# Small recurrence products as 64-column tiles, and expert tiles of 80 slots

## The reference, cut to what matters

```python
def moe_swiglu(xn, w_router, w_gate, w_up, w_down):
    xt = xn.reshape(-1, d)                        # 256 rows
    logits = (xt @ w_router).astype(jnp.float32)
    top_vals, top_idx = lax.top_k(logits, TOP_K)  # 2 of 8 experts
    ...
    for e in range(N_EXPERTS):                    # widths 1024 -> 3584 -> 1024
        y = y + combine[:, e:e + 1] * swiglu(xt, w_gate[e], w_up[e], w_down[e])

def step(state, inp):                             # the recurrence, a state of 64 x 64 per head
    sa = jnp.einsum('bhvk,bhk->bhv', state, -kk_t)
    state = (state * w_t[:, :, None, :] + sa[..., None] * (kk_t * a_t)[:, :, None, :]
             + v_t[..., None] * k_t[:, :, None, :])
    return state, jnp.einsum('bhvk,bhk->bhv', state, r_t)
```

## Time and profile before

| | |
|---|---|
| median of 3 runs | 3103.71 us (3098.95 to 3111.47) |
| the profiled execution | 3109.32 us, its span 3107.6 us |
| TensorE busy | 2872.6 us, 92% of the span |
| TensorE weight loads busy | 2470.1 us, 79% |
| VectorE, ScalarE busy | 795.6 us, 427.0 us |
| mean granted clock | 0.943 |
| read from device memory | 568.79 MB |

### The profile page before, as it was taken

One profiled execution on the slowest core, in us unless ns is written; L12 is line 12 of the kernel. 1 busy time (PEld: TensorE's weight loads), 2 busy tenths in 40 slices (PEclk: granted clock), 3 DMA queues, 4 the chain that ended last, 5 costly groups with the idle time before them and its releaser, 6 DMA issues. The chain is left out here.

```text
span 3107.6 us, 71912 instructions
## 1 busy us (share of the span) xinstructions
PE 2872.6 (92%) x31985; PEld 2470.1 (79%) x31985; DVE 795.6 (26%) x1962; ACT 427.0 (14%) x941; POOL 84.3 (3%) x144
## 2 busy tenths in 40 slices
PE   8798999979799999999999898999788999997998
PEld 6687776768699999999999777665677889896665
DVE  5412000621201101101110123000436766763001
ACT  1101000111101100101000122000023222221000
POOL 0100000000000000000000000000000000001000
PEclk9899999989899999999999976999898988988999
DMA  6334445433399999999999630645300000001442
GB/s 211 121 110 136 149 149 159 142 109 127 110 399 381 390 408 390 388 407 389 389 407 390 220 109 7 204 156 191 115 19 4 3 3 2 2 2 61 143 154 95
DMA packets 291364, 571.02 MB, mean 184 GB/s; under 512 B 18182, under 2 KB 181764, under 8 KB 291284
## 3 DMA queue, kind: packets, MB, share of 16 engines
q1 hardware_dynamic: 291284, 569.92, 50.9%
HBM read 568.79 MB, written 5.28 MB: 185 GB/s over the span
## 5 line engine op out<-in xcount | busy, mean ns | idle before, releaser
L1604 PE MATMUL ps<-xg,ring 128*64 128x88 f32 x14336 | 549.7, 239 | 1.1 <-issue 1.1
L1604 PEld LDWEIGHTS ps<-xg,ring 128*64 128x64 f32 x14336 | 545.7, 137 | 2.8 <-issue 2.8
L1199 PE MATMUL ps<-xT,ring 128*128 128x256 f32 x1728 | 386.0, 383 | 5.2 <-PEq L445 2.5
L1199 PEld LDWEIGHTS ps<-xT,ring 128*128 128x128 f32 x1728 | 332.5, 193 | 68.7 <-issue 22.0
L1211 PE MATMUL ps<-ring,hidden 128*128 128x512 f32 x688 | 301.8, 592 | 0.0
L1620 PE MATMUL ps<-hidden,expert_down 128*64 128x88 f32 x7168 | 277.8, 239 | 2.1 <-issue 2.1
L1620 PEld LDWEIGHTS ps<-hidden,expert_down 128*64 128x64 f32 x7168 | 274.2, 137 | 2.5 <-issue 2.5
L1211 PEld LDWEIGHTS ps<-ring,hidden 128*128 128x128 f32 x688 | 130.7, 190 | 147.5 <-issue 145.4
L610 PE MATMUL ps<-ring,xT 128*128 128x256 f32 (+1 forms) x1056 | 229.0, 380 | 8.0 <-PEq L1080 5.5
L610 PEld LDWEIGHTS ps<-ring,xT 128*128 128x128 f32 x1056 | 198.8, 196 | 36.7 <-issue 9.7
L610 PE MATMUL ps<-xT,ring 128*128 128x256 f32 (+1 forms) x944 | 212.9, 387 | 9.9 <-PEq L588 4.5
(11 more groups left out here) (354 smaller groups left out, 2641.7 us busy)
## 6 DMA issues: line engine op xcount, KB each, us to landing
ring<-in_moe_w_gate_dram SPq DMA_DIRECT2D x128, 896.0 KB, 8.8
ring<-in_moe_w_up_dram SPq DMA_DIRECT2D x128, 896.0 KB, 9.5
expert_down<-in_moe_w_down_dram SPq DMA_DIRECT2D x96, 1024.0 KB, 10.0
ring<-in_mlp_w_dram SPq DMA_DIRECT2D x64, 1024.0 KB, 5.4
ring<-in_w_xkv_dram SPq DMA_DIRECT2D x16, 1024.0 KB, 5.3
expert_down<-in_moe_w_down_dram SPq DMA_DIRECT2D x32, 512.0 KB, 10.2
ring<-in_ffn_w_gate_dram SPq DMA_DIRECT2D x11, 1024.0 KB, 5.3
ring<-in_ffn_w_up_dram SPq DMA_DIRECT2D x11, 1024.0 KB, 5.3
```

Of the source, the lines that this page charges most:

```text
L1199: mm = pe.matmul(bank[:, m * SEQ:(m + 1) * SEQ], w[:, c, m * P:(m + 1) * P], self.xT[:, c, :], start=(c == 0), stop=(c == KC - 1))
L1604: mm = pe.matmul(bank[b][o:o + HEAD, at, :], w[:, c, f * P + o:f * P + o + HEAD], xg[:, p * E_STEP + c, :], start=(p == 0 and c == 0 and a ...
```

## The change

Three things change.
- The small products of the recurrence are made in halves of 64 output partitions each with 64 columns of weights (`by_halves`, which the kernel has). For the new state only the half that is used later is made, and the order of its four products is changed.
- The first products of a pair are issued in another order: `Bs` for both heads, then `Ks` for both heads.
- An expert tile has 80 slots where it had 88. `MAX_TILES` becomes 4, `VIRTUAL` 32 and `MAX_ITEMS` 14. The early loads of the first chunk stay as they are.

```diff
-SLOTS = 88
+SLOTS = 80
...
-                                b = ps[:, 4 * d + 2 * t + hh, :]
-                                pe.matmul(b[:, 0:2 * P], Bs[d][half(hh), t, :], both, start=True, stop=True)
-                                pe.matmul(b[:, 2 * P:4 * P], Ks[d][half(hh), t, :], both, start=True, stop=True).then_inc(q["products_done"].sem, 1)
+                                pe.matmul(ps[:, 4 * d + 2 * t + hh, 0:2 * P], Bs[d][half(hh), t, :], both, start=True, stop=True)
+                            for hh in range(2):
+                                both = KR[d][half(hh), t].rearrange("p a b -> p (a b)")
+                                pe.matmul(ps[:, 4 * d + 2 * t + hh, 2 * P:4 * P], Ks[d][half(hh), t, :], both, start=True, stop=True).then_inc(q["products_done"].sem, 1)
...
-                                pe.matmul(ps[:, 4 * d, 0:P], KR[d][:, t, 0, :], S0[d][:].rearrange("p a b -> p (a b)"), start=True, stop=False)
+                                by_halves(pe, ps[:, 4 * d, 0:P], KR[d][:, t, 0, :], S0[d][:].rearrange("p a b -> p (a b)"), start=True, stop=False)
                             for hh in range(2):
-                                mm = pe.matmul(ps[:, 4 * d, hh * HEAD:(hh + 1) * HEAD], GM[d][:, 2 * t + hh, 2, :], vc[:, t, half(hh)],
+                                mm = by_halves(pe, ps[:, 4 * d, hh * HEAD:(hh + 1) * HEAD], GM[d][:, 2 * t + hh, 2, :], vc[:, t, half(hh)],
                                                start=(step == 0), stop=(step == 0 or hh == 1))
...
-                                mm = pe.matmul(ps[:, 4 * d + 1, hh * HEAD:(hh + 1) * HEAD], XT[d][:, 2 * t + hh, :], rhs[d][:, hh, :], start=True, stop=True)
+                                mm = by_halves(pe, ps[:, 4 * d + 1, hh * HEAD:(hh + 1) * HEAD], XT[d][:, 2 * t + hh, :], rhs[d][:, hh, :], start=True, stop=True)
...
-                                for hh in range(2):
-                                    dst = ps[:, 4 * d + 3, 256 + hh * HEAD:256 + (hh + 1) * HEAD]
-                                    pe.matmul(dst, rowsBK[d][:, 0, :], sa[d][:, t, hh, :], start=True, stop=False)
-                                    mm = pe.matmul(dst, rowsBK[d][:, 1, :], vc[:, t, half(hh)], start=False, stop=True)
+                                for n in range(2):
+                                    for hh in range(2):
+                                        dst = ps[half(hh), 4 * d + 3, 256 + hh * HEAD:256 + (hh + 1) * HEAD]
+                                        mm = pe.matmul(dst, rowsBK[d][:, n, half(hh)], vc[:, t, half(hh)] if n else sa[d][:, t, hh, :], start=(n == 0), stop=(n == 1))
                                 mm.then_inc(q["state_done"].sem, 1)
                             if step:
-                                pe.matmul(ps[:, 4 * d + 2, t * P:(t + 1) * P], KR[d][:, t, 1, :], S0[d][:].rearrange("p a b -> p (a b)"), start=True, stop=False)
+                                by_halves(pe, ps[:, 4 * d + 2, t * P:(t + 1) * P], KR[d][:, t, 1, :], S0[d][:].rearrange("p a b -> p (a b)"), start=True, stop=False)
                             for hh in range(2):
                                 dst = ps[:, 4 * d + 2, (2 * t + hh) * HEAD:(2 * t + hh + 1) * HEAD]
-                                pe.matmul(dst, GM[d][:, 2 * t + hh, 1, :], sa[d][:, t, hh, :], start=(step == 0), stop=False)
-                                mm = pe.matmul(dst, GM[d][:, 2 * t + hh, 3, :], vc[:, t, half(hh)], start=False, stop=(step == 0 or hh == 1))
+                                by_halves(pe, dst, GM[d][:, 2 * t + hh, 1, :], sa[d][:, t, hh, :], start=(step == 0), stop=False)
+                                mm = by_halves(pe, dst, GM[d][:, 2 * t + hh, 3, :], vc[:, t, half(hh)], start=False, stop=(step == 0 or hh == 1))
```

## The result

| | before | after |
|---|---|---|
| median of 4 runs each | 3107.06 us (3098.95 to 3111.47) | 3030.60 us (3027.06 to 3033.83) |
| ratio | | 0.9757, 95% interval 0.9730 to 0.9783 |
| the profiled execution | 3109.32 us | 3028.41 us, its span 3026.7 us |
| mean granted clock | 0.943 | 0.949 |

A forecast was written before the change was run, and what follows sets the result against it. TensorE was taken to bound the expert stage by only 3% over the load queue. Experts 39.2 + small products 18.4 + clock 17 = 74.6 us, taking 3109.3 to 3034.7, or 3029 beside the median; range 3010 to 3062.

The forecast's parts named there:

- The record of the expert lines: Expert stage: a TensorE record moving 80 columns in place of 88 falls from 37.9 to 34.5 ns.
- Rival (b): Expert stage: records do not shorten because 64-column weight loads set the pace; whole kernel at 3068 us, chance 0.07.
- The queue takes over at 407 GB/s: Expert stage: TensorE's item falls to 102.2 us, below the load queue's 108.2 us, so loads set the pace.
- The breaks: Expert stage, between items: they cost nothing more; TensorE, 9.4 us late after one, catches up in the third chunk.
- Rival (c): Expert stage: the queue follows TensorE past 407 GB/s, saving 74 us, not 39; whole kernel at 2994 us, chance 0.05.
- The end of the stage: Expert stage: the down products end at 1692.6 us in place of 1731.8, 39.2 us less.
- Five us per item idle for DMA: Expert stage: TensorE's profile rows for L1604 and L1620 should show some 5 us per item of idle time released by DMA.
- The small section: Recurrence: section 8.3 us, clean pair 53.2 us; 2.3 us less in each of eight pairs, 18.4 us in all.
- The clock: Recurrence: falls of the granted clock in the small sections cost less; 17 us won, bounds 10 lost to 21 won.
- Rival (a): Recurrence: the clock falls as often or more, so the 17 us become 0; whole kernel at 3046 us, chance 0.20.
- Order of the first products: Recurrence: issuing `Bs` for both heads, then `Ks`, changes nothing, as both heads' `Bs` already run side by side; 0 us.
- Rival (d): Expert stage: the clock falls as TensorE waits for loads; slower, 3192 us if for half the stage's time, chance 0.04.

The follow-up runs named there:

- slots84: The kernel after with 84 expert slots in place of 80; 3035.06 us, ratio 0.9772 to the kernel before.
- slots80_alone: The kernel before with expert tiles of 80 slots in place of 88 and nothing else; 3069.99 us, ratio 0.9873.
- after_again: The kernel after, unchanged, measured once more in a second comparison; 3034.42 us, ratio 0.9770 to the kernel before.
- state_first_again: The kernel after with VectorE's scaling of the new state moved before the last two parts of its factor work, measured again; 3026.40 us, ratio 0.9744.
- state_first_before: The kernel before with VectorE's scaling of the new state moved before the last two parts of its factor work; 3105.82 us, ratio 1.0001.
- half_loads_88: The kernel before with each gate and up load behind the first chunk bringing only half its piece; 3103.38 us, ratio 0.9994.
- tiles_alone: The kernel after with 88 expert slots again, so only the recurrence is changed; 3068.72 us, ratio 0.9876 to the kernel before.
- wide_moves: The kernel before with the recurrence's `sa` and state products moving 128 columns, of which 64 are used; 3089.62 us, ratio 0.9941.
- order_alone: The kernel before with only the new order of `Bs` and `Ks` in a pair's first products; 3107.28 us, ratio 0.9991.

## Why the prediction was right

**The record of the expert lines: right.** 34.5 ns was predicted, 34.6 measured, 36.2 with 84 slots. For two records side by side these are 69.2 and 72.4 ns, as the 75.8 before some 2.5 ns more than two cycles of the full clock for each column. Rival (b), the weight load as the pace of a 64-column tile, falls.

**The queue takes over at 407 GB/s: right.** The item was to take 108.2 us and took 108.18; the dip between items is gone. The cause is shown from both sides by the two kernels with half loads: the same relief gives 38 us at 80 slots and nothing at 88. `slots84`, where TensorE's 106.9 us an item lie just under the queue's 108.2, gives all but 2.2 us of the gain. The breaks cost nothing more, as predicted: TensorE meets the late loads from the third chunk of an item on, once two items have used up the slack. Rival (c) was right in its price of 74 us and wrong in its premise: with a longer queue the rate stays at 407. The 435 GB/s that the Trainium skill gives for the ports ("DMA: Bandwidth & Descriptors", "Where 436 GB/s comes from") was reached in no window shown here.

**The end of the stage: the term is off by 3.5 us.** 39.2 us less was predicted and 35.7 measured. The end itself, 1692.6, was near to 1693.7, but only because the stage began 2.2 us earlier than before, where the sum has it 1.0 later. By the sum the stage lasts 845.6 us; it lasted 849.9. Of these 4.3 us 1.3 stand in front of the first load, 2.2 between its issue and the last landing (844.1 us, where the sum has 3.3 of loss and 838.6), and 0.8 behind the last landing (2.1, not 1.3). The first load is issued 3.7 us into the stage (847.48 - 843.79), not 2.6 less the 0.2 that the sum gave back: the first piece's records run at a granted clock of 0.65 in the first 2.2 us and 0.53 in the next 2, where the kernel before had 1.00. Window and timeline of after:

```profile
843.80:860.00 16.20, 15.16 (x385) 15.05 (x387) 0.92 (x5) 1.98 (x3) 0.00 (x0) 0.89 0.65 233
```
```profile
843.79 13.90 PE L1604 MATMUL ps<-xg,ring 128*64 128x80 f32 x348 [1.03 <-issue]
858.73 3.68 PE L1604 MATMUL ps<-xg,ring 128*64 128x80 f32 x100 [1.04 <-issue]
...
864.68 4.64 PE L1620 MATMUL ps<-hidden,expert_down 128*64 128x80 f32 x127 [1.30 <-issue]
870.93 2.58 PE L1620 MATMUL ps<-hidden,expert_down 128*64 128x80 f32 x69 [1.61 <-issue]
873.34 1.89 PE L1604 MATMUL ps<-xg,ring 128*64 128x80 f32 x49
```

The clock is 0.89 and the rate 233 GB/s in the first 16 us, where 1.00 and 257 had been read before. The first chunk has 4.0 us of idle time put down to issue (2.3 before) and ends at 873.34, 29.6 us after its start where a free one takes 23.3. A stage of 850 us was measured in `slots80_alone` and `after_again` too, so that this is no chance of one execution, while the 2.2 us of the earlier start are. The low clock at the start stands in all six profiles with 80 slots and in three of the six with 88; why was not settled.

**Five us per item idle for DMA: right in the sum, wrong in the row.** The groups show only 7.1 and 11.2 us of idle time in front of L1604 and L1620 for the whole stage, though its items take 6 us longer than TensorE's work. The gap between two records is too short to show: a record is in flight for 233 ns, and a wait of 0.2 us between two of them can leave TensorE busy. In the waiting fourth chunk the next line starts 1360.60 - 1342.13 = 18.47 us after the first of 448 records. Less the 0.17 and 0.47 us that are shown as idle these are 17.83 us, 39.8 ns each against 34.6, so by this estimate some 2.3 us of this wait stand in no idle row. The Trainium skill, "Perfetto Trace Analysis", opens by calling matmul busy time a bad metric because matmuls are pipelined; here the 500 us window reads 486.88 busy, 97%, in a stage whose TensorE has 5% to spare (811.8 of 849.9 us). Not foreseen was that L1620 waits for VectorE too: `hidden` is made in 0.45 us behind the late piece, some 0.48 us in each waiting chunk.

**The small section: right.** 8.3 us predicted, 8.28 to 8.45 measured, 2.35 less than before in each of seven; the clean pair 53.2, measured 53.20 to 53.22. The record came to 29 ns where 27.6 was taken. By the Trainium skill, "TensorE: Matmul & The Clock Gate", "Wait — 56ns, not 53.3ns?", starts are never closer than 25 ns however few columns move, and the trace agrees as far as it goes; the 62 ns of its other decode mode, by which nothing would have been won, do not hold here. That the chain behind ScalarE and VectorE sets the new length was predicted, with VectorE's start as its first link, and `state_first_again` shows it: taking that link away gives 1.2 us more per pair. What the sum overlooked is the eighth section: no next pair's factor work stands in front of VectorE there, and up to the last start of its `S,used` products it became 3.6 us shorter (9.60 to 6.04). Together the sections give 7 x 2.35 + 3.6 = 20.0 us, not 18.4.

**The clock: right in direction, mis-sized.** 17 us were taken between bounds of -10 and 21. The recurrence as a whole became 40.0 us shorter; less the 20.0 of the sections as they run at full clock, 20.0 are the clock's, near the bound of 21 for the case in which all three long falls go. The falls themselves, sections of 17.24 us where 10.80 is full clock, are 3 x 6.4 = 19.3 of it. The 17 us were a choice within wide bounds, with no mechanism behind it that a row of before showed; that it came near is luck in part. The falls are absent in all seven profiles of kernels that have the tiles and present in four of the five other profiles with 128-column small products that move 64 columns (three falls in three of them, two in `state_first_before`). `half_loads_88` has none, loses some 7 us elsewhere in its pairs instead, and is 12 us shorter there than the kernel before; so some 12 of the 20 us can come or go in a single execution without the change. That the change removes the falls is what the seven profiles bear out, and with them the times of `tiles_alone`, 38 us less where the sections alone give 20. `wide_moves` shows that the products need not become cheaper for it. What in these sections makes the clock fall was not settled. Rival (a) did not come.

**Order of the first products: right,** by `order_alone`. Rival (d), half clock in the expert stage, did not come: the clock reads 1.00 in the window of 500 us, through all waits. It fell twice in the stage for a few us, both times behind a break and not in a wait: in the first 4 us of the stage and at the start of the seventh item (1486.78 us), where it reads 0.57 over 3.2 us and the gate and up products of the first chunk took 16.87 us in place of 15.54.

**Sum.** 39.2 + 18.4 + 17 had been 74.6; measured 35.7 + 20.0 + 20.0 = 75.7, and 5.2 more outside the two stages. The errors of -3.5, +1.6 and +3.0 us have opposite signs and let the total fall closer than its terms: that part is luck. So is some of the nearness of 3029 to 3030.6, since the forecast starts from a median of 3103.7 of three runs, and the kernel before then read 3107.1. (The four chances of times below 3088 us add up to 0.94, not 0.93.)

## What to carry to other kernels

Before a tile is cut, price the loads beside it: when both engines look full, a backlog that grows within a loop and is worked off in its breaks tells that the queue is the next bound and how near, and one experiment with half the bytes tells what it will keep. A small product can cost what its weights' columns cost and not what it moves: here a float32 record with 128 columns of weights took 112 ns for 64 moved columns, and two halves side by side took 58 for the same, in spite of twice the records. And after shortening one engine's part of a chain, look at what the others do just before their link: work put there when it was hidden is now on the path.

## What the runs showed of the hardware that was not expected

- In the expert stage the queue moves 407 GB/s whether a load takes some 10 us from issue to landing, as in the window 997 to 1062 before, or 16.5 as after. The Trainium skill, "HBM Reference", "Specifications (TRN2)", gives 358 GB/s as a core's share with its neighbour streaming and about 425 for a core alone; this core had 406 or 407 in every window shown here in which the queue was never empty.
- 64-column float32 tiles side by side start 29 ns apart when they move 64 columns, where one with 128 columns of weights takes 112 ns and, by `wide_moves`, hardly more when it moves 128 columns.
- The same instructions can lose 12 us more or less to the granted clock from one profile to the next: seven pairs took 414.75 and 402.50 us. With equal data too, 13 runs of the kernel before took 3091.8 to 3112.9 us at mean clocks of 0.947 and 0.941.
- With 84 slots the load queue was busy at 407 GB/s for 500 us on end and still did not hold TensorE back: a queue that is always busy need not be the bound.
